# Latent attention: mask in VectorE's maximum pass, two heads' values side by side, packed PSUM tiles, probabilities scaled on GpSimd

## What is computed

```python
s = (einsum("bqhd,bkhd->bhqk", qn, k_nope) + einsum("bqhr,bkr->bhqk", qp, k_pe)) * MLA_SCALE
s = where(kpos <= qpos, s, -1e30)
p = softmax(s, axis=-1)
o = einsum("bhqk,bkhd->bqhd", p, v)          # then o @ w_o
```

## Time and profile before

| | |
|---|---|
| median of 3 runs | 2253.02 us (2251.74 to 2259.87) |
| the profiled execution, its own time | 2254.11 us |
| span in its profile | 2252.0 us |
| PE busy, of the span | 2121.6 us, 94% |
| POOL busy | 1441.2 us, 64% |
| DVE busy | 1173.8 us, 52% |
| ACT busy | 562.7 us, 25% |
[...]
| chain that ended last | PE 78%, DVE 15%, ACT 3% |
| latent attention, first score to first matmul of `mla_o` | 1576.7 to 1707.7 us |

### The profile page before, as it was taken

How to read it: one execution, slowest core, us unless ns; L and a number is a source line. 1 busy time by engine, 2 the same in 40 slices (tenths; PEclk the granted TensorE clock), 3 DMA queues, 4 the chain that set the end, 5 groups by cost and what they waited for, 6 DMA issues and landing times.

```text
span 2252.0 us, 25804 instructions
## 1 busy us (share of the span) xinstructions
PE 2121.6 (94%) x9472; PEld 1685.9 (75%) x9472; DVE 1173.8 (52%) x1639; ACT 562.7 (25%) x1054; POOL 1441.2 (64%) x667
## 2 busy tenths in 40 slices
PE   7998897999999789799999999997899999999997
PEld 5676776888888678576888888876556868888886
DVE  4349855423435799763732332568666346313234
ACT  4233343221111314322210111233442132101011
POOL 6415336877877669682887778775004828777774
PEclk9998998999999899999999999998999999999999
DMA  4102022322222235221232223222001203223221
GB/s 176 53 24 66 29 76 97 112 94 94 96 94 94 82 112 171 89 87 38 85 103 94 96 92 100 80 85 88 19 1 43 99 24 103 98 94 101 95 87 63
DMA packets 55464, 187.75 MB, mean 83 GB/s; under 512 B 6080, under 2 KB 7872, under 8 KB 55264
## 3 DMA queue, kind: packets, MB, share of 16 engines
q1 hardware_dynamic: 50976, 179.07, 24.0%
q10 hardware_dynamic: 4384, 7.21, 1.0%
HBM read 183.37 MB, written 2.10 MB: 82 GB/s over the span
## 4 chain that ended last, share of the span: by engine, by line
PE 78%; DVE 15%; ACT 3%; issue 2%; POOL 1%; DMA 0%; SPq 0%; DVEq 0%; ACTq 0%; POOLq 0%
PE bank L545 23%; PE bank L547 23%; PE bank L546 23%; DVE bank L2035 3%; PE bank L905 2%; PE bank L1108 1%; ACT EM L1598 1%; PE bank L1088 1%; PE bank L830 1%; PE bank L750 1%; POOL wH L504 1%; PE bank L702 1%; DVE MIX L1731 1%; DVE qkL L1909 1%; PE bank L599 1%
## 5 line engine op out<-in xcount | busy, mean ns | idle before, releaser
L504 POOL TENSOR_TENSOR wH<-raw,zero 128x1024 fp32r<-128x1024 f32 (+2 forms) x317 | 613.5, 1935 | 733.8 <-PE bank L547 726.1
L507 POOL TENSOR_TENSOR wL<-raw,wH 128x1024 fp32r<-128x1024 f32 (+2 forms) x317 | 761.9, 2404 | 24.9
L545 PE MATMUL bank<-hnH,wH 128*128 128x512 f32 (+1 forms) x1472 | 588.8, 400 | 49.8 <-DVE hnL L1646 32.8
L547 PE MATMUL bank<-hnH,wL 128*128 128x512 f32 (+1 forms) x1472 | 581.6, 395 | 0.0
L546 PE MATMUL bank<-hnL,wH 128*128 128x512 f32 (+1 forms) x1472 | 581.5, 395 | 0.0
L545 PEld LDWEIGHTS bank<-hnH,wH 128*128 128x128 f32 (+1 forms) x1472 | 279.4, 190 | 121.2 <-DVE hnL L1646 38.1
L546 PEld LDWEIGHTS bank<-hnL,wH 128*128 128x128 f32 (+1 forms) x1472 | 279.9, 190 | 62.1 <-issue 2.0
L547 PEld LDWEIGHTS bank<-hnH,wL 128*128 128x128 f32 (+1 forms) x1472 | 279.2, 190 | 62.5 <-issue 0.8
L545 PE MATMUL bank<-actH,wH 128*128 128x512 f32 x784 | 308.8, 394 | 1.2 <-DVE actL L2090 1.2
L547 PE MATMUL bank<-actH,wL 128*128 128x512 f32 x784 | 305.3, 389 | 0.0
L546 PE MATMUL bank<-actL,wH 128*128 128x512 f32 x752 | 292.5, 389 | 0.0
(11 more groups left out here) (328 smaller groups left out, 2618.0 us busy)
## 6 DMA issues: line engine op xcount, KB each, us to landing
raw<-weights SPq DMA_DIRECT2D x315, 512.0 KB, 3.4
raw<-weights SPq DMA_DIRECT2D x28, 384.0 KB, 3.0
XT<-x_t SPq DMA_DIRECT2D x8, 256.0 KB, 6.8
XT<-x_t ACTq DMA_DIRECT2D x1, 2048.0 KB, 8.3
out<-MIX ACTq DMA_DIRECT2D x8, 256.0 KB, 2.2
memT<-mem_t ACTq DMA_DIRECT2D x1, 1024.0 KB, 5.3
KC<-KC ACTq DMA_DIRECT2D x3, 256.0 KB, 3.9
CT<-consts ACTq DMA_DIRECT2D x1, 552.0 KB, 5.6
```

The costliest lines, as they stand in the source:

```text
L504: nc.gpsimd.tensor_tensor(wH[:, slot, 0:w], raw[:, slot, 0:w], nothing.broadcast_to([P, w]), ALU.add)\
L507: nc.gpsimd.tensor_tensor(wL[:, slot, 0:w], raw[:, slot, 0:w], wH[:, slot, 0:w].bitcast(F32), ALU.subtract).then_inc(split, 1)
L545: mm(out_, aH, bH, start=first, stop=False)
L547: return mm(out_, aL, bH, start=False, stop=last)
```

## The change

PE: the mask matmuls (and `identR`, `neg_futureR`, two copies of DVE at the start, and the semaphore for them) are gone. The scores of a head lie in three tiles: block 3 (512 columns), blocks 2 and 0 (384 + 128), block 1 (256). The turned probabilities lie in three tiles as well, by key block, and `PX2` holds four heads without the unused columns. The values of heads 2p and 2p+1 are multiplied together, matmul by matmul in turns, into the two halves of one tile. Scores have banks 0 to 2, turned tiles 3 to 5, values 6 and 7 in turn. The second half of `mla_v` moves into the first three iterations. DVE: `reduce_max` becomes a `tensor_tensor_reduce` that adds `not_past` (zeros and minus 1e30) to the scores in place, scales by minus the scale, and takes the minimum; the reciprocals come in three pieces. POOL: the multiplication by the reciprocal, between its split of `mla_o` 1 and of `mla_o` 2.

```diff
+        for _n in range(MLA_HEADS + 2):
+            if _n < MLA_HEADS:
+                TILES += [("score", range(3 * _n, 3 * _n + 3))]
+            TILES += [("mla_v", {0: (4, 5), 1: (6,), 2: (7,)}.get(_n, ()))]
+            if _n >= 3 and _n % 2:
+                TILES += [("value", ((_n - 3) // 2,))]
+            if 1 <= _n <= MLA_HEADS:
+                TILES += [("turn", range(3 * _n - 3, 3 * _n))]
+        TILES += [("mla_o", 8)]
+        OWN_BANKS.update({"q_turn": [1, 2, 7, 0], "mla_v": [3, 4, 5, 6, 6, 7, 6, 7], "score": [0, 1, 2] * MLA_HEADS,
+                          "turn": [5, 3, 4] * MLA_HEADS, "value": [6, 7] * (MLA_HEADS // 2)})
...
+SCORE_AT = ((0, 3, 0, 0), (1, 2, 0, 1), (1, 0, 3, 2), (2, 1, 0, 3))
+TURN_AT = ((1, 0), (2, 0), (0, 0), (2, 3))
+ROWS_AT = (0, 512, 1024, 896)
...
+            def probabilities(h):
+                for t, b, _, o in SCORE_AT:
+                    probs = EM[:, h % 2, b, 0:(b + 1) * P]
+                    if o != 2:
+                        pool.wait_ge(sig("m_inverse"), 3 * h + t + 1)
+                    nc.gpsimd.tensor_tensor(probs, probs, mst[:, h % 2, 8 + o:9 + o].broadcast_to([P, (b + 1) * P]),
+                                            ALU.mult).then_inc(sig("m_probs"), 1)
+
             for u0, n, w, kind, _ in runs:
                 i0 = 0
+                if u0 == POS["mla_o", 2]:
+                    for h in range(MLA_HEADS):
+                        probabilities(h)
...
             def att_scores(h):
...
-                    mm(psum(n)[:, 0:w], QC[0:96, h, b * P:b * P + P], KC[0:96, h, 0:w], start=True, stop=False)
-                    mm(psum(n)[:, b * P:w], identR[:, :], neg_futureR[:, :], start=False, stop=True).then_inc(tile_done, 1)
+                    last = mm(psum(n)[:, c0 * P:c0 * P + w], QC[0:96, h, b * P:b * P + P], KC[0:96, h, 0:w], start=True,
+                              stop=True)
+                    if o != 1:
+                        last.then_inc(tile_done, 1)
...
+            def att_values(pair):
+                n = TILE0["value"] + pair
                 claim(n)
+                for h in (2 * pair, 2 * pair + 1):
+                    for t in range(3):
+                        gone_wait(pe, TILE0["turn"] + 3 * h + t)
+                gone_wait(pe, TILE0["mla_v"] + (3 if pair < 4 else 7))
                 for j in range(NB):
-                    last = mm(psum(n)[rows, j * P:], VL[:, j, h * 64:h * 64 + 64], PX2[:, h % 2, j, j * P:],
-                              start=(j == 0), stop=(j == NB - 1))
+                    for i in range(2):
+                        h = 2 * pair + i
+                        last = mm(psum(n)[64 * i:64 * i + 64, j * P:], VL[:, j, h * 64:h * 64 + 64],
+                                  PX2[:, h % 4, ROWS_AT[j]:ROWS_AT[j] + S - j * P], start=(j == 0), stop=(j == NB - 1))
                 last.then_inc(tile_done, 1)
...
             for i in range(MLA_HEADS + 2):
                 if i < MLA_HEADS:
                     att_scores(i)
-                if i >= 2:
-                    att_values(i - 2)
+                for b in {0: (0, 1), 1: (2,), 2: (3,)}.get(i, ()):
+                    later_value(b)
+                if i >= 3 and i % 2:
+                    att_values((i - 3) // 2)
                 if 1 <= i <= MLA_HEADS:
                     att_turn(i - 1)
...
+            def att_probs(h):
+                for t, b, c0, o in SCORE_AT:
+                    n = TILE0["score"] + 3 * h + t
+                    if o != 2:
+                        act.wait_ge(sig("m_max"), 3 * h + t + 1)
+                    w = (b + 1) * P
+                    last = run(EM[:, h % 2, b, 0:w], psum(n)[:, c0 * P:c0 * P + w], ACT.Exp,
+                               bias=mst[:, h % 2, o:o + 1], scale=-1.0, accum_out=mst[:, h % 2, 4 + o:5 + o])
+                    if o != 1:
+                        free(last, n)
...
+            nc.vector.memset(not_past[:, 0:S - P], 0.0)
+            link(nc.vector.tensor_copy(not_past[:, S - P:], neg_future))
...
+            def att_max(h):
+                for t, b, c0, o in SCORE_AT:
+                    n = TILE0["score"] + 3 * h + t
+                    if o != 2:
+                        tile_wait(dve, n)
+                    w = (b + 1) * P
+                    own = psum(n)[:, c0 * P:c0 * P + w]
+                    last = nc.vector.tensor_tensor_reduce(own, own, not_past[:, S - w:], -scale, BIG, ALU.add, ALU.min,
+                                                          mst[:, h % 2, o:o + 1])
+                    if o != 1:
+                        last.then_inc(sig("m_max"), 1)
+
+            def att_inverse(h):
+                for t, cols in enumerate((slice(0, 1), slice(1, 3), slice(3, 4))):
+                    gone_wait(dve, TILE0["score"] + 3 * h + t)
+                    nc.vector.reciprocal(mst[:, h % 2, 8 + cols.start:8 + cols.stop],
+                                         mst[:, h % 2, 4 + cols.start:4 + cols.stop]).then_inc(sig("m_inverse"), 1)
...
+            for i in range(MLA_HEADS + 2):
+                if i < MLA_HEADS:
+                    att_max(i)
+                    att_inverse(i)
+                if i >= 3 and i % 2:
+                    att_low((i - 3) // 2)
+                if 1 <= i <= MLA_HEADS:
+                    if i >= 5:
+                        tile_wait(dve, TILE0["value"] + (i - 5) // 2)
                     att_rows(i - 1)
```

More of the change, by code:

```diff
@@ L187 @@
         TILE_DONE[_t] = ("unit", POS["pc_out", 3 + _i // 2 if _i < 6 else _i] + 1)
-    elif _n == "b_v" and _i < 3:
+    elif _n == "b_v" and _i < 3 or _n == "mla_v" and 4 <= _i < 7:
         _others += 1
@@ L461, in program @@
             kind = "memory" if u in MEMORY else ""
-            if runs and runs[-1][2:] == [w, kind, ahead]:
+            if runs and runs[-1][2:] == [w, kind, ahead] and u != POS["mla_o", 2]:
                 runs[-1][1] += 1
@@ L1070, in _ @@
             turn_positions(2)
[L1071 to L1075, removed]
+            project_natural("mla_v", cH[:, 3:5, :], cL[:, 3:5, :], 2, NB, TILE0["mla_v"], POS["mla_v", 0], 1)
+            turn_positions(3)
             for b in range(NB):
@@ L1078, in _, with later_value @@
             gone_wait(pe, TILE0["k_turn"])
+            def later_value(b):
+                u, n = POS["mla_v", 1], TILE0["mla_v"] + 4 + b
+                pe.wait_ge(split, u + 1)
+                claim(n)
+                tok = slice(b * P, b * P + P)
+                for k in range(2):
+                    cut = slice(k * S, k * S + S)
+                    last = three(psum(n)[:, :], cH[:, 3 + k, tok], cL[:, 3 + k, tok], wH[:, u % RING, cut],
+                                 wL[:, u % RING, cut], k == 0, k == 1)
+                last.then_inc(unit_done if b == NB - 1 else tile_done, 1)
             def att_scores(h):
@@ L1559, in position_rows, with latent_value @@
                 free(last, n)
[L1561 to L1565, removed]
+            def latent_value(g, b):
+                n = TILE0["mla_v"] + 4 * g + b
+                tile_wait(act, n)
+                free(run(VL[:, b, g * S:g * S + S], psum(n)[:, :], ACT.Copy, scale=rcq[:, 4 + b:5 + b]), n)
@@ L1574, in att_rows @@
             def att_rows(h):
-                for b in (0, 2):
-                    n = mtile("t", h, b)
+                for t, j in ((0, 2), (1, 0)):
+                    n = TILE0["turn"] + 3 * h + t
                     tile_wait(act, n)
[L1578 to L1581, removed]
@@ L1583, in att_high @@
-            def att_high(h):
-                n = mtile("o", h, 0)
+                    w = S - j * P
+                    free(run(PX2[:, h % 4, ROWS_AT[j]:ROWS_AT[j] + w], psum(n)[:, 0:w], ACT.Copy), n)
+            def att_high(pair):
+                n = TILE0["value"] + pair
                 tile_wait(act, n)
-                if h == 0:
+                if pair == 0:
                     act.wait_ge(sig("k_copied"), 16 * 3)
-                rows = slice(64 * (h % 2), 64 * (h % 2) + 64)
-                run(oHL[rows, h // 2 * 2, :], psum(n)[rows, :], ACT.Copy).then_inc(sig("m_hi"), 1)
@@ L1591, in _ @@
[L1591 to L1594, removed]
-                    if i >= 2:
[L1596 to L1602, removed]
+                run(oHL[:, 2 * pair, :], psum(n)[:, :], ACT.Copy).then_inc(sig("m_hi"), 1)
@@ L2271, in _, with att_low @@
-            att_low(MLA_HEADS - 2)
-            att_rows(MLA_HEADS - 1)
-            att_low(MLA_HEADS - 1)
+            def att_low(pair):
+                n = TILE0["value"] + pair
+                dve.wait_ge(sig("m_hi"), pair + 1)
+                free(tt(oHL[:, 2 * pair + 1, :], psum(n)[:, :], oHL[:, 2 * pair, :].bitcast(F32), ALU.subtract), n)
+            def att_max(h):
+                for t, b, c0, o in SCORE_AT:
+                    n = TILE0["score"] + 3 * h + t
+                    if o != 2:
+                        tile_wait(dve, n)
[5 more added lines that the diff above has]
+                        last.then_inc(sig("m_max"), 1)
```

103 lines of the change are left out of this document (33 added, 70 removed).

## The result

| | before | after |
|---|---|---|
| median, four executions each | 2255.35 us (2251.74 to 2259.87) | 2206.80 us (2206.69 to 2208.26) |
| the profiled execution, its own time | 2254.11 us | 2206.82 us |
| span | 2252.0 us | 2204.9 us |
| first score, first matmul of `mla_o` | 1576.7, 1707.7 us | 1577.9, 1660.4 us |

The ratio of the times is 0.9784, 95% interval 0.9769 to 0.9799: 2.2% faster. The profiled executions differ by 47.3 us, and the first matmul of `mla_o` comes 47.3 us earlier: all of the gain in these two executions lies in the stage.

The account below looks back on a forecast made before the run. A per-head ring of waits through PE, ACT and DVE (7.69 us, PE's own work 6.3) was taken as the bound. Sixteen heads 79.2, mla_v 5.6, idle 4.8, clock 2.2, end 2.0: 93.8 against 136.6, so 2210 us; own range 2202 to 2218, stated 2202 to 2232.

Parts of the forecast that it names:

- The ring of the earlier trace is cut: Attention stage: waits from score block 3 through ACT and DVE's low part, about 1.4 us a head, end with separate banks.
- Masks gone: PE's scores: without mask matmuls four scores cost between 1.9 and 2.56 us a head, taken as 2.2.
- Two heads side by side: PE's values: two heads alternate on column halves of the array; a pair takes 2.3 us, bounds 2.3 and 4.6.
- The rival's price: Values one after the other: a pair takes 4.6 us, 18.4 comes back, 2228.6; chance 0.18.
- One pass for maximum and mask: DVE's new reduction reads each column once: 0.68 us for 512 columns, 1.95 a head; two passes would be 3.9.
- GpSimd: Probabilities scaled on POOL instead of DVE: 2.9 us a head taken, between 2.5 and 5.3.
- The cover of 1.8: Probabilities ready about 6.3 us after a head's scores begin, PE asks at 8.1, so POOL's work is covered by 1.8.
- Start: Stage start: mla_v's second half no longer covers ACT's position_rows(3); PE stands from 1571.1 to 1575.9, 4.8 us lost.
- The clock's price: Stage start: a slow PE clock after the idle gap costs 2.2 us more.
- Hand-overs and transposes: PE, each head: ten transposes 1.4 us plus 0.2 for hand-overs (0 to 0.5).
- Slower: Whole kernel: the changed kernel measures slower than before; chance 0.05.
- No change: Whole kernel: a ring of equal length through POOL leaves 7.7 us a head, 2250; chance 0.05.

Follow-up runs that it names:

- banks and moved parts: Kernel before with separate banks for scores, turned tiles and values, and high and low parts moved behind copies and multiplications: 2265.73 us, ratio 1.0040.
- the move alone: Kernel before, banks unchanged, with ScalarE's high part moved behind its copies and VectorE's low part behind the scaling of probabilities: 2249.24 us, ratio 0.9964.
- banks_lists_blocks: Kernel before with separate banks, moved high and low parts, and each block's maximum scaled and handed to ScalarE by itself: 2246.66 us, ratio 0.9955.

## Why the prediction was right, and where not

2210 was forecast, 2206.8 came: a gain of 47.3 in the profiled executions instead of 42.8. By its steps:

- **"The ring of the earlier trace rows is cut" by banks of their own: this step was wrong, and the forecast came out in spite of it.** Banks alone (bank 4 used twice) leave the period at 7.68. What set the pace before was the circle of VectorE and ScalarE; I had taken a step of the chain for a wait that it isn't. The forecast held since I had added up PE's own work, and since other parts of the change, planned for other reasons, broke the circle: that is luck as far as the mechanism goes. What shortened it when added is the handing over of maxima in pieces (0.81 a head, on top of banks and moved parts; the move alone 0.13). That banks matter once the circle is shorter is seen in that kernel's chain, where the values wait for theirs.
- **Masks gone**: 2.2 a head taken, 2.16 measured; 0.10 a mask by the run that puts them back, so that a saving of nothing is excluded.
- **Two heads side by side**: 2.3 a pair, measured 2.30, and taking it back costs 1.56 a pair. The rival's price, 18.4, was too high: in turn the pair takes 3.86, not 4.6. The 2.9 a pair in the forecast's upper end (2218) was shown by no row of before, and no run shows it: the runs gave 2.30 alternating, 16 passes in the time of 8 or 2.0 times the rate, and 3.86 in turn.
- **One pass for maximum and mask**: 695 ns for 512 columns against 678 for the plain maximum, so one pass. An accumulator read of 142 behind each I had not counted; starts lie 0.61, 0.51, 0.25 and 0.39 apart, 1.8 a head by the timeline, so it costs next to nothing.
- **GpSimd**: 1041 + 828 + 613 + 400 = 2.88 busy, 2.9 taken. The cover of 1.8 held with a microsecond more a head, and was gone with 2.9 more. On VectorE the same four multiplications take 1.27 a head (L2272 in VectorE's timeline of the banks of their own), yet scaling there makes the stage 9.3 us longer. Some 4.8 of it come in around two SBUF operations held beside GpSimd's split (4.08 for both, 0.61 elsewhere), as one was in the earlier trace rows (2.60, and 0.42 without it), and by the steady period it costs 0.25 a head. The reciprocals were not held (162 ns in the mean, beside GpSimd's multiplications).
- **Start**: the first score at 1575.9 forecast, 1577.9 measured. The idle 4.8 I had (4.75), but not that PE waits 1.1 ahead of it, for bank 5: with the new banks `mla_v`'s third tile follows a tile of `q_nope` that VectorE empties late. The other 0.9 I have not traced. The clock's price, 2.2, was right: head 0's scores took 4.61 at clock 0.50 (1577.87 to 1582.48), head 1's 2.32.
- **Hand-overs and transposes, 1.6 a head: the term mis-sized.** It measured 1.09 and, behind values, 1.24: 4.48 a head against 4.95, 7.5 us over sixteen heads. Less the start's 2.0 and some 1 us elsewhere, that is the 4.5 by which the forecast was short. The 1.4 for ten transposes was the duration of their group; I should have used distances between starts, as for the scores.
- **Slower (0.05)** fell: the clock was 1.00 in all steady windows, 1592 to 1656. No run shows the change's steady part at the low clock. **No change** fell for the kernel as a whole, but with the banks alone a ring of equal length is what was left.

## What to carry to other kernels

When a chain of waits shows a ring, check each of its steps against the kernel: does the engine really wait there for what the chain names? Then write down the lists of all engines for one period and look for a ring whose steps leave no slack. Here the banks looked like the cause and, put in alone, were worth nothing, and the timeline of the kernel before held the true ring all along. Its mark was two engines that wait for each other in turns (2.83 and 4.44 us idle in a period), and handing over in smaller pieces shortened it. And an edit is worth what the limit of the day lets it be: the same masks cost 0.4 us by the stage before, where the medians show no change, and 8 us after.

## What the hardware showed that I had not expected

- Two column halves of the array on float32 passes ran fully at once: 16 passes in 2.30 us, as 8 did. With the halves in turn, two passes at the border still overlapped (3.86, not 4.60).
- Two SBUF-to-SBUF `TENSOR_SCALAR` of VectorE took 1.79 and 2.37 us beside GpSimd's split (0.61 for both elsewhere), where a `RECIPROCAL` in SBUF, started 0.1 us into the same split, kept its 0.17.
- With banks alone the first score, behind a wait of 2.60 us, came 2.8 us later against the rotation, the clock was 0.50 from 1592 to 1600 (0.88 before), and the first values came 7.4 later. The same wait of 2.60 stands ahead of the first score of banks_lists_blocks, with the clock at 1.00 from 1592 to 1608 (0.65 with banks alone).
